# A two-layer diffusion trunk on one core: the Hyena transforms and filter spectra by four token classes instead of two

## The reference

```python
h = h * jnp.exp(-t[:, None] * deltas)[:, None, None, :]
full = jnp.concatenate([h[:, :, 0], jnp.zeros((1, HY_ORDER, HY_W), F32), h[:0:-1, :, 1]], 0)
spec = jnp.fft.rfft(full, axis=0)
...
def long_conv(z, o):
    y = jnp.fft.irfft(jnp.fft.rfft(z, n=2 * n, axis=1) * spec[None, :, o, :], n=2 * n, axis=1)[:, :n]
    return y + z * bias[o]

z = x1 * long_conv(v, 0)
z = x2 * long_conv(z, 1)
return z * jax.nn.silu(gate)
```

## Time and profile before

| | us |
|---|---|
| median of 3 runs | 2919.62 |
| the runs | 2919.88, 2899.03, 2919.62 |
| span of the profiled execution | 2913.2 |

### The profile page before, as it was taken

One profiled execution on the slowest core, in us unless ns is written; L12 is line 12 of the kernel. 1 busy time (PEld: TensorE's weight loads), 2 busy tenths in 40 slices (PEclk: granted clock), 3 DMA queues, 4 the chain that ended last, 5 costly groups with the idle time before them and its releaser, 6 DMA issues.

```text
span 2913.2 us, 50304 instructions
## 1 busy us (share of the span) xinstructions
PE 2752.0 (94%) x21254; PEld 2160.7 (74%) x21254; DVE 1542.9 (53%) x2691; ACT 1008.1 (35%) x1640; POOL 640.3 (22%) x261
## 2 busy tenths in 40 slices
PE   7999998999999999999999999888899999999997
PEld 1387877887788888887787448777776787887775
DVE  4646676425624443436747644667524554352856
ACT  0335443312222343224432134544332233432533
POOL 0022000121123211320124312100132342142036
PEclk9999999999999999999999999999999999999999
DMA  7521000323332112220134651000233331232034
GB/s 230 173 78 43 16 19 24 107 77 116 96 118 87 59 51 103 79 80 30 48 109 157 199 185 58 30 14 14 74 109 119 128 129 55 89 121 69 23 116 166
DMA packets 104958, 261.95 MB, mean 90 GB/s; under 512 B 11202, under 2 KB 33860, under 8 KB 104352
## 3 DMA queue, kind: packets, MB, share of 16 engines
q1 hardware_dynamic: 94314, 231.07, 24.1%
q10 hardware_dynamic: 10422, 27.67, 2.6%
HBM read 217.27 MB, written 34.08 MB: 86 GB/s over the span
## 4 chain that ended last, share of the span: by engine, by line
PE 77%; DVE 13%; ACT 4%; DMA 3%; issue 3%; POOL 1%; DVEq 0%; SPq 0%; ACTq 0%
PE ps L823 17%; PE ps L824 16%; PE ps L825 16%; PE ps L1003 4%; PE ps L831 4%; PE ps L1330 4%; PE ps L962 2%; PE ps L1269 2%; PE ps L1357 2%; PE ps L840 2%; DVE t_gcv L1979 1%; PE ps L1340 1%; PE ps L917 1%; PE ps L946 1%; DMA t_raw<-in_w_ada 1%
## 5 line engine op out<-in xcount | busy, mean ns | idle before, releaser
L784 POOL TENSOR_TENSOR t_wlo<-t_raw,t_whi 128x1024 fp32r<-128x1024 f32 x248 | 618.5, 2496 | 2242.0 <-ACT t_whi L1451 2242.0
L823 PE MATMUL ps<-t_u_hi,t_whi 128*128 128x512 f32 (+1 forms) x2368 | 862.4, 364 | 10.5 <-issue 4.1
L824 PE MATMUL ps<-t_u_lo,t_whi 128*128 128x512 f32 (+1 forms) x2368 | 834.6, 352 | 0.0
L825 PE MATMUL ps<-t_u_hi,t_wlo 128*128 128x512 f32 (+1 forms) x2368 | 831.2, 351 | 0.0
L1451 ACT ACTIVATE t_whi<-t_raw 128x1024 fp32r<-128x1024 f32 x248 | 262.4, 1058 | 890.9 <-PE ps L825 687.4
L823 PEld LDWEIGHTS ps<-t_u_hi,t_whi 128*128 128x128 f32 x2368 | 449.8, 190 | 83.1 <-issue 18.2
L825 PEld LDWEIGHTS ps<-t_u_hi,t_wlo 128*128 128x128 f32 x2368 | 448.0, 189 | 63.3
L824 PEld LDWEIGHTS ps<-t_u_lo,t_whi 128*128 128x128 f32 x2368 | 450.1, 190 | 58.5 <-issue 3.4
L1522 ACT ACTIVATE t_grp<-ps 128x512 f32<-128x512 f32 (+2 forms) x236 | 104.3, 466 | 228.7 <-PE ps L840 107.0
L2514 DVE TENSOR_REDUCE t_amx<-ps 128x1 f32<-128x768 f32 (+1 forms) x120 | 101.5, 846 | 149.2 <-PE ps L1330 148.6
L1971 DVE TENSOR_TENSOR t_yv<-t_oT,t_sil 128x768 f32<-128x768 f32 (+1 forms) x32 | 67.1, 2097 | 184.2 <-ACT t_sil L1522 184.2
(11 more groups left out here) (267 smaller groups left out, 3865.7 us busy)
## 6 DMA issues: line engine op xcount, KB each, us to landing
t_raw<-in_w_in SPq DMA_DIRECT2D x184, 512.0 KB, 3.6
t_raw<-in_w_ada SPq DMA_DIRECT2D x48, 512.0 KB, 4.4
t_raw<-in_w_br SPq DMA_DIRECT2D x32, 512.0 KB, 3.6
t_raw<-in_w_out SPq DMA_DIRECT2D x32, 512.0 KB, 4.2
t_sg<-gate_logits SPq DMA_DIRECT2D x28, 384.0 KB, 4.2
hs<-t_hstage ACTq DMA_DIRECT2D x20, 512.0 KB, 3.6
t_hring<-hs SPq DMA_DIRECT2D x20, 512.0 KB, 6.6
t_raw<-in_fwd SPq DMA_DIRECT2D x64, 128.0 KB, 3.0
```

Of the source, the lines that this page charges most:

```text
L784: pool.tensor_tensor(wlo[:, c % CONV, :], raw[:, s % RAW, :], whi[:, c % CONV, :].bitcast(f32), ALU.subtract).then_inc(sems["w_ready"], 1)
L823: pe.matmul(o, lh, rh, start=first, stop=False)
L824: pe.matmul(o, lh, rl, start=False, stop=False)
L825: return pe.matmul(o, ll, rh, start=False, stop=last)
```

## The change

The tokens of the latent stream are divided by their number modulo 4, and the channels into two halves of 256. A round m now does all frequencies of one half of the channels. `forward(m)` has eight products of 256 columns, where there were eight of 512; `inverse(m)` has 16 products of 128 columns, where there were 16 of 256. In exchange VectorE adds and subtracts over twice as many steps (`apart`, `together`). The filter spectra of a latent group take eight products in the first step as before, and four in the second in place of eight; its even and odd sums are kept in `eb`. The context stream is computed as before. The tables stand in buffers of their own, loaded once for the spectra and once for the convolutions of each layer, and leave the common stream. Both projections of the next two tiles stand ahead of the second inverse, and the gate tiles use banks 6 and 7 alone.

```diff
     yield "inv", 0, 0
     yield "next", 0, 0
+    yield "next", 0, 1
     yield "inv", 0, 1
...
-                    else:
-                        s += [(kind, st, m)]
-            s += [("w", first[2] + P * j) for j in range(1, 4)] + gates[:1]
+                        s += [("w", first[o + 1] + P * m)]
...
+            htab = sb("htab", [P, CLASS, 2, P], stack=m)
+            hinv = sb("hinv", [P, 2, LAT], stack=m)
+            hctab = sb("hctab", [P, 2 * CTX], stack=m)
+            hcinv = sb("hcinv", [P, 2 * CTX], stack=m)
...
+            if nt == LT:
+                return x[:, base + b:base + LAT:CLASS]
+            return parity_block(x, base, nt, b)
...
-            n = len(segs(l == 0))
-            conv = (6, 7)[2 - n:] + (2, 3)[2 - n:] * 2
-            return conv + conv + (6, 7)[2 - n:]
+            return (6, 7)
...
+            def class_table(dst, name):
+
+                x = A["fwd"][0].rearrange("(q r) (c k f) -> q r c k f", r=CLASS, c=2, k=LT)
+                for k in range(LT):
+                    load(dst[32 * k:32 * k + 32, :, :, :], x[:, :, :, k, :], name)
...
+                    if kind == "ada" and (a, b) == (2, 0):
+                        if l:
+                            sp.wait_ge(sems["wo_h"], NT)
+                        class_table(ftab, "ld_ftab")
+                        if l == 0:
+                            parity_table(fctab, "ld_ftab")
...
+            def terms(bank, *parts):
+
+                for n, (table, x) in enumerate(parts):
+                    last = pe.matmul(ps[:, bank, :], table, x, start=n == 0, stop=n == len(parts) - 1)
+                return last
...
+            def spectrum_of(s, b):
+
+                if b == 0:
+                    claim(2, 3)
+                    for e in range(2):
+                        last = terms(2 + e, (ftab[:, 2, e, :], s[:, e, 2, :]))
+                    ln.done(last, "f_fo")
+                    lend("f_oc", 2, 3)
+                    claim(0, 1)
+                    for e in range(2):
+                        last = terms(e, (ftab[:, 0, e, :], s[:, e, 0, :]))
+                    ln.done(last, "f_ev")
+                    lend("hy_ps", 0, 1)
+                    claim(2, 3)
+                    for e in range(2):
+                        last = terms(2 + e, (ftab[:, 1, e, :], s[:, e, 1, :]), (ftab[:, 3, e, :], s[:, e, 3, :]))
+                    ln.done(last, "f_ev")
+                    lend("f_stage", 2, 3)
+                    return
+                claim(0, 1)
+                terms(0, (ftab[:, 1, 1, :], s[:, 0, 1, :]), (ftneg[:, 0, :], s[:, 0, 3, :]))
+                ln.done(terms(1, (ftneg[:, 1, :], s[:, 1, 1, :]), (ftab[:, 3, 0, :], s[:, 1, 3, :])), "f_ev")
+                lend("f_stage", 0, 1)
...
+                def forward(m):
+
+                    for lo, name, reader in ((2, "f_fo", "hy_oc"), (0, "f_ev", "hy_ps")):
+                        claim(lo, lo + 1)
+                        for r in range(lo, lo + 2):
+                            for e in range(2):
+                                last = pe.matmul(ps[:, r, e * 256:e * 256 + 256], htab[:, r, e, :],
+                                                 z[:, r, m * 256:m * 256 + 256], start=True, stop=True)
+                        ln.done(last, name)
+                        lend(reader, lo, lo + 1)
+
+                def inverse(m, i):
+
+                    claim(4 + 2 * m, 5 + 2 * m)
+                    for x in range(2):
+                        for r in range(CLASS):
+                            for e in range(2):
+                                y0 = AT_CLASS[r][e] * 256 + x * P
+                                last = pe.matmul(ps[:, 4 + 2 * m + x, r * P:r * P + P], y[:, i % 2, y0:y0 + P],
+                                                 hinv[:, e, r:LAT:CLASS], start=r == 0 and e == 0,
+                                                 stop=r == CLASS - 1 and e == 1)
+                    ln.done(last, "hy_iv")
+                    for x in range(2):
+                        lend("hy_inv", 4 + 2 * m, 5 + 2 * m)
...
-                project(full, "cv_done")
+                for j in range(2):
+                    project(full, "cv_done")
                 for o in range(2):
-                    for j in range(1, 4):
+                    for j in range(2, 4):
                         project(full, "cv_done")
-                        to_tok(o, j - 1, freed["cv_done"] - 1)
+                        to_tok(o, j - 2, freed["cv_done"] - 2)
                     for _ in range(gate_units(l)):
                         next(gates)
-                    to_tok(o, 3, freed["cv_done"])
+                    to_tok(o, 2, freed["cv_done"] - 1)
+                    to_tok(o, 3, freed["cv_done"], nslot[0] % 2)
                     ln.take("hy_z", 4)
+                    if o == 0:
+                        pe.wait_ge(sems["ld_ftab"], 16 * (27 if l else 18))
...
+                        elif m:
+                            ln.take("hy_iv")
+                            ln.take("hy_y", len(streams(l)) + 1)
+                            for j in range(2):
+                                results(0, j)
...
+                def apart(i):
+
+                    t = y[:, i % 2, :].rearrange("p (g w) -> p g w", g=8)
+                    two = y[:, i % 2, :].rearrange("p (a b w) -> p a b w", a=2, b=2)
+                    if i >= 2:
+                        dve.wait_ge(sems["hy_iv"], i - 1)
+                    tt(two[:, 0, :, :], ps[:, 0:2, :], h_odd[:, :, :], ALU.add)
+                    ln.step(tt(two[:, 1, :, :], ps[:, 0:2, :], h_odd[:, :, :], ALU.subtract), "hy_ps")
+                    tt(hv8[:, 0:3:2, :], t[:, 0:5:4, :], t[:, 2:8:5, :], ALU.add)
+                    tt(hv8[:, 1:4:2, :], t[:, 0:5:4, :], t[:, 2:8:5, :], ALU.subtract)
+                    tt(hv8[:, 4:8:3, :], t[:, 1:6:4, :], t[:, 3:7:3, :], ALU.add)
+                    step(tt(hv8[:, 5:7, :], t[:, 1:6:4, :], t[:, 3:7:3, :], ALU.subtract))
+
+                def together(i):
+
+                    o = y[:, i % 2, :].rearrange("p (g w) -> p g w", g=8)
+                    tt(hv8[:, 0:4, :], oT[:, :, 0:256], oT[:, :, 256:512], ALU.add)
+                    tt(hv8[:, 4:8:3, :], oT[:, 0:2, 0:256], oT[:, 0:2, 256:512], ALU.subtract)
+                    step(tt(hv8[:, 5:7, :], oT[:, 2:4, 0:256], oT[:, 2:4, 256:512], ALU.subtract))
+                    tt(o[:, 0:2, :], hv8[:, 0:4:2, :], hv8[:, 1:4:2, :], ALU.add)
+                    tt(o[:, 2:4, :], hv8[:, 0:4:2, :], hv8[:, 1:4:2, :], ALU.subtract)
+                    tt(o[:, 4:6, :], hv8[:, 4:6, :], hv8[:, 6:8, :], ALU.add)
+                    ln.step(tt(o[:, 6:8, :], hv8[:, 4:6, :], hv8[:, 6:8, :], ALU.subtract), "hy_y")
```

More of the change, by code:

```diff
@@ L233, in stream_of @@
             s += [("ada", a, b)]
-        if kind == "blk":
-            s += [("fwd", int(l == 0 and a < 2), b)]
     for n, b in enumerate(BRANCHES):
@@ L549, in source @@
                 return A["w_br"][l, a[0], a[1]]
[L550 to L553 removed]
+            return A["w_out"][l, a[0], a[1]]
         def chunk(t, d):
@@ L1274, in hyena @@
[L1274 removed]
+                            if st:
+                                inverse_ctx(spectra[0])
+                            else:
+                                inverse(m, spectra[0])
                             spectra[0] += 1
[L1276 to L1279 removed]
+                for j in range(2, 4):
@@ L2416, in hyena @@
                     for kind, st, m in convolution(l):
+                        if kind in ("gate", "next"):
+                            ln.skip(1)
                         if kind != "fwd":
-                            ln.skip(1)
                             continue
```

330 lines of the change are left out of this document (189 added, 141 removed).

## The result

The changed kernel takes 2962.97 us (median; 2956.72 to 2968.95), the kernel before 2917.27 beside it. The ratio is 1.0167, with a 95% interval of 1.0129 to 1.0204: 1.7% slower. The prediction was 2933 us, in a range of 2888 to 2966: the sign and the range hold, but the loss is 46 us where 13 were forecast. The profiled execution has a span of 2965.2 us, 52.0 over that of before.

The account below looks back on a forecast made before the run. TensorE, busy 94% of the span, was taken as the bound. Layer 1 +5.9, layer 0 -3.4, openings -6.1 and clock +16.9 gave +13.3 us on a 2913.2 us span; with 6.4 for the median, 2933 us, range 2888 to 2966.

Parts of the forecast that it names:

- wait for the taps: Behind the second inverse: TensorE waits for ScalarE's copies and the taps, 3.5 us uncovered in layer 1.
- A round with two collisions: VectorE's latent round in layer 1: 18.1 us alone, 22.2 us with two GpSimd splits beside it.
- VectorE takes the gain back: Layer 1's convolutions: VectorE's longer rounds make TensorE wait, all gain there goes into three waits, sum +5.9 us.
- VectorE isn't the bound: Rival for the convolutions: new additions hidden or cheap, a round stays at 14.3 us, about 2863 us in all; chance 0.16.
- from 7.25 to 3.63 us: -29 us: Term for the eight latent inverses on TensorE: time follows the columns, so each takes 3.63 us.
- reading every fourth column is slower: Rival for the inverse's table: strided reads take twice the time, +19 us, 2952 us; chance 0.05.
- The wait for the second `y`: Layer 1, before the second inverse: TensorE ready at 41.0 us, `y` at 48.2 us, wait 7.1 us.
- the table DMAs: Layer 0's opening: eight table DMAs ahead of weight tile (2, 0) cost between 0 and 7 us, taken as +2.5.
- the low bound: Behind each long TensorE pause: 3.3 us at half clock, 1.7 us lost; the high bound was 10 us, 5 lost.
- The clock holds: Rival for the new pauses: the clock holds or comes back at once, -3.6 us, 2916 us; chance 0.17.
- Stays low for long: Rival for the ten new pauses: some 10 us at half clock behind each, +28 us more, 2961 us; chance 0.20.
- the sum for the clock: Half clock behind TensorE's new waits: layer 1 +10.2, layer 0 +5.0, openings +1.7, together +16.9 us.

Follow-up runs that it names:

- v1: e1 with seven VectorE operations a round left out in each layer's second convolution (output not the reference's): 2946.23 us, one execution.
- e1: Changed kernel with the latent inverse table stored class by class, so the inverse reads 128 adjoining columns: 2956.75 us, ratio 1.0157.
- e2: Changed kernel with the four inverse places reading table columns at distances 1, 2, 3 and 4 (output not the reference's): 2955.89 us, one execution.
- e3: Changed kernel with ScalarE's first middle tap back behind the first projection at the start of each layer's Hyena branch: 2949.5 us, ratio 1.0149.
- c1: The changed kernel itself measured a second time, with no edit: 2958.36 us, ratio 1.0161.
- e4: Changed kernel with layer 0's eight opening table DMAs issued ahead of weight tile (3, 1) in place of (2, 0): 2953.39 us, ratio 1.0151.
- w1: Changed kernel with products of no use filling TensorE's new waits: 2969.04 us, ratio 1.0200.
- b5: b1 with the taps of the two tiles projected ahead of the second inverse no longer behind that inverse: 2910.48 us, ratio 0.9996.
- b6: b5 with a gate tile moved into layer 1's first wait and other waits for y filled with products of no use: 2897.33 us, ratio 0.9953.
- b1: Changed kernel with the edits of e1, e3 and e4, and other banks for the second half of a spectrum's first step: 2930.24 us, ratio 1.0051.

## Why the prediction came out as it did

**What held.** The forwards, the waits and who ends them. Layer 1: first `y` 25.5 us after the first forward (26.0 forecast), wait 7.39 (7.5), wait for the taps 4.22 (3.5). Layer 0: first `y` at 35.5 (36.3) with a wait of 3.40, and 5.73 in the second convolution, where VectorE meets a split more (4.3 forecast for both); taps 5.47 (4.7). A round with two collisions is 21.5 us (22.2); an operation of 512 elements took 0.62 us, where 0.70 was taken. The collision itself, in the timelines of DVE and POOL, the same three operations beside a split and without one:

```profile
2237.15 4.57 DVE L2090 TENSOR_TENSOR t_hcv<-t_oT 128x1024 f32<-128x1024 f32 x3
2238.57 2.60 POOL L818 TENSOR_TENSOR t_wlo<-t_raw,t_whi 128x1024 fp32r<-128x1024 f32 x1 [6.31 <-ACT t_whi L1550]
2256.64 2.43 DVE L2090 TENSOR_TENSOR t_hcv<-t_oT 128x1024 f32<-128x1024 f32 x3
```

That VectorE takes the gain back was the core of the forecast, and v1 shows it; "VectorE isn't the bound" is refuted.

**What failed: the inverse.** The term "from 7.25 to 3.63 us: -29 us" was worth nothing. I weighed it as a rival, "reading every fourth column is slower", with 0.05 and a price of 19 us, on the ground that every second column costs nothing. That row was no evidence for four. e1 and e2 show the cost, and where it fell: 11 us in layer 0. In layer 1 it was hidden, since the inverse fills time in which VectorE isn't ready. The wait for the second `y` was 0.9 us instead of 7.1: TensorE came 3.0 us later than forecast (43.97 us after the first forward, not 41.0), and `y` 3.3 us earlier (44.9, not 48.2), as its round met one split and not two. The Trainium skill, "Advanced Engine Details and Errata", section "SBUF Cachelines", says that on-chip memory is read in lines of 16 bytes and that full speed takes at least two hits on a line. Columns of 4 bytes at distance 2 give two hits, at distance 4 one: the trace agrees with 3.8 against 7.5 us, and I should have weighed that rule before giving 0.05. At distance 3 four columns lie on three such lines, and the 0.172 us of e2 are three quarters of 0.227; so an estimate, worked out from these times and the 16 bytes that the Trainium skill states there, is 1.8 ns for each line touched, wherever that is more than TensorE needs for its columns.

**Waits that the sum left out.** Before each layer's first convolution the third projection waits for its slot too, 4.69 and 3.44 us: I took it as covered, as it was, and did not see that ScalarE's first tap had moved behind the second projection (e3: 14 us with the clock). In the opening the table DMAs were put at 2.5 us within bounds of 0 and 7; the wait grew by 8.9 us (7.4 in c1), over the upper bound (e4). And the first step of a spectrum waits for ScalarE's copy of banks 2 and 3, 1.53 us in layer 0 and 1.99 in layer 1, which no term had. The 2.61 us behind it were forecast (2.5).

**The clock: mechanism right, place wrong.** All ten pauses of 3.4 us or more in the convolutions and at their start ended at half clock, in both profiles of the changed kernel. The stretches at half behind them last 2.9 to 6.2 us by the granted clock, where 3.3 was taken as the low bound. Two of them:

```profile
757.30:760.30 3.00, 3.00 (x9) 2.52 (x10) 2.89 (x5) 0.00 (x0) 0.00 (x0) 0.50 0.00 0
760.30:763.30 3.00, 3.00 (x12) 2.61 (x11) 1.31 (x2) 0.00 (x0) 0.00 (x0) 0.55 0.03 5
763.30:766.30 3.00, 3.00 (x19) 2.61 (x18) 0.00 (x0) 0.00 (x0) 0.00 (x0) 1.00 0.00 0
...
720.20:725.20 5.00, 5.00 (x22) 5.00 (x23) 4.93 (x7) 1.82 (x3) 0.61 (x1) 0.50 0.84 324
```

A third projection takes 11.24 and 10.59 us for 8.64 in layer 0 and 7.14 and 7.29 for 5.72 in layer 1: 7.5 us for the four (5.9 in c1; 6.8 forecast), and w1 gives them back. "The clock holds" is refuted. The first inverses paid nothing (last row: 22 records in 5 us at half, as at full), because the read of every fourth column limits them at either clock; the forecast had charged layer 0's with 0.8 us each, and layer 1's second inverses, which ran at full clock, with 3.4 each.

"Stays low for long" didn't come behind the ten, but it did in the openings. Behind the pause of 2.61 us that was forecast there, the clock stood at half for 13.6 us, in layer 0 of the first profile and in layer 1 of c1:

```profile
111.10:124.70 13.60, 13.60 (x17) 2.78 (x16) 7.68 (x16) 3.03 (x4) 0.00 (x0) 0.50 0.18 62
```

```profile
1693.40:1707.00 13.60, 13.60 (x16) 2.71 (x15) 5.97 (x10) 0.59 (x2) 0.00 (x0) 0.50 0.28 102
```

Busy time times lacking clock is 15.7 us in c1's two openings and 6.8 before: 9 us, where the forecast had 1.7. So the sum for the clock, 16.9 us, is near what c1 shows (57 us without the latent inverses, 43 before) by luck. Two readings of the trace before were too rough for it. Most pauses there were not followed by half clock: leaving out the wait ahead of the first instruction, TensorE had 17 pauses of 1.4 us or more, and behind 5 of them the clock was at half within 2.2 us. And its 18 stretches at half were not nearly all near 3.3 us: 10 were of 3.4, the others of 6.8 to 12.8.

**The account**, by c1's trace (span 2956.5, 43.3 over before), each part timed between the same instructions:

| part | forecast | measured |
|---|---|---|
| convolutions up to the third projection, layer 0 / 1 | -4.3 / +10.1 | +8.1 / +6.0 |
| from there to the next first forward, layer 0 / 1 | +11.9 for all four | +2.7 / +2.6, first ones |
| both together | +17.7 | +19.4 |
| opening of layer 0 / 1 | -4.4 together | +7.0 / +4.4 |
| opening to first forward, layer 0 / 1 | 0 | +6.9 / +5.6 |
| all else | 0 | about 0 |

The forecast of the convolutions is near by luck. Up to the third projection it was 12.4 us too low in layer 0, of which 11 are the inverse, and 4.1 too high in layer 1, where the second `y` came early. Behind the third projection it was too high again; there the second convolutions have no next forward, and their share (third projections 2.9 us slower in c1) is in "all else". Nearly all of the 30 us between forecast and result lie outside, in the openings and the start of the branch. In the two openings c1 shows 11 us less work at full clock (14.1 forecast), 13 us more idle time of TensorE and 9 us more clock.

**What stays open.** The total of e1 moved by less than its trace shows, and between b5 and b6 by more; stretches that no edit touches (the part between layer 0's convolutions and layer 1's opening: 793 to 803 us) differ that much between executions. Why the clock stays at half for 13.6 us behind a pause of 2.61 us and for less behind longer ones is open too. Parts of b6's gain may be had by the kernel before as well; that wasn't tried.

## What to carry to other kernels

When an operand is cut into classes, store its table class by class: halving the columns is worth nothing if the remaining ones, of 4 bytes here, lie four apart. Before counting work that leaves the bound engine, lay out by hand when each helper will be ready, in every place where the moved step stands, the first one too; here the engine that took over the additions gave back all of layer 1's gain. What stands behind the last operation of a chain on a helper (here two taps) can often be done before it; here that gave 20 us (b1 to b5), more than any other single edit.

## What the runs showed of the hardware

- A moving operand (the one that streams through TensorE) of 128 columns of 4 bytes takes 0.112 us at distance 1, 0.115 at 2, 0.172 at 3 and 0.227 at 4, at full clock (e1, e2). At half clock it takes 0.213 at distances 1 and 3, and 0.227 at 4.
- GpSimd's split lengthened VectorE's work beside it by 2.0 to 2.1 us each time, three times in a convolution of layer 1 of the changed kernel; moving TensorE's work earlier moves these meetings too (four in e1).
- Ten pauses of TensorE of 3.4 to 7.4 us all ended at half clock, which lasted 2.9 to 6.2 us from the first product behind them; in w1, with 0.8 to 1.2 us of pause left ahead of the third projections, these ran at full clock.
